# Tile 0's front of a hybrid decoder step: products of 128 and 256 columns replaced by products of 512 columns over pairs of weight chunks

## What is computed

```
mod  = silu(c) @ w_ada + b_ada                      # six rows of 1024 for each of nine conditions
h    = rmsnorm(x, g1) * (1 + scale1) + shift1
proj = h @ w_in                                     # 7 x 1024 columns: q, k, v, u, gv, gate a, gate b
out_b = stick_breaking_attention(q, k, v)           # 8 heads x 128, causal
out_a = gelu(u) * (tril(w_s) @ layernorm(gelu(gv)) + b_s)
merged = sigmoid(gate_a) * (out_a @ w_ba) + sigmoid(gate_b) * (out_b @ w_bb)
x    = x + gate1 * (merged @ w_out)
h2   = rmsnorm(x, g2) * (1 + scale2) + shift2
q2   = h2 @ w_query                                 # 8 heads, two halves of 128
s    = q2 . sub_keys  -> top 16 of each half -> best 16 of the 256 pairs = 16 experts per head
y    = rmsnorm(x + gate2 * sum_k softmax_k * gelu(h2 . down[e_k]) * up[e_k])
```

## Time and profile before

| | |
|---|---|
| median of three timed runs | 2341.11 us |
| the profiled execution: device time | 2341.77 us |
| the profiled execution: span, first to last instruction | 2340.0 us |
| mean granted TensorE clock | 0.838 |
| busy: PE, DVE, POOL, ACT | 73%, 70%, 35%, 34% |
| DMA | 841.14 MB, mean 359 GB/s |

### The profile page before, as it was taken

The page is one execution under the profiler, slowest core; times in us unless marked ns, Lnnn a source line. Parts: engine busy times, 40 slices in busy tenths (PEclk is TensorE's granted clock), DMA queues, the critical chain, the costliest instruction groups (busy, mean ns, idle before and its releaser), DMA issues.

```text
span 2340.0 us, 22796 instructions
## 1 busy us (share of the span) xinstructions
PE 1712.1 (73%) x7010; PEld 1189.8 (51%) x7010; DVE 1630.5 (70%) x3454; ACT 802.8 (34%) x2085; POOL 814.7 (35%) x647
## 2 busy tenths in 40 slices
PE   6998957988889666878777763766460677777776
PEld 2747956845778555644475752765450222222111
DVE  1011168748898878877985968888989866766764
ACT  1121013386345123238413213452122334443332
POOL 0000024324343324434433423443345444444432
PEclk9999978978989787987655586888685899999989
DMA  7786879977989979997896998999999999999997
GB/s 232 277 259 228 299 305 422 421 299 286 410 343 421 393 283 422 418 421 272 345 417 261 412 365 328 375 420 369 363 412 354 390 420 420 421 415 416 378 387 300
DMA packets 129310, 841.14 MB, mean 359 GB/s; under 512 B 15487, under 2 KB 20863, under 8 KB 33882
## 3 DMA queue, kind: packets, MB, share of 16 engines
q0 software_dynamic: 86512, 615.29, 65.3%
q1 hardware_dynamic: 37348, 217.83, 24.8%
q10 hardware_dynamic: 5328, 6.56, 0.8%
HBM read 824.39 MB, written 15.22 MB: 359 GB/s over the span
## 4 chain that ended last, share of the span: by engine, by line
DMA 28%; PE 27%; DVE 22%; ACT 8%; issue 7%; DVEq 5%; ACTq 1%; POOL 1%; SPq 0%; POOLq 0%
DMA gather_ring<-in_experts,expert_numbers 27%; PE bank L749 10%; PE bank L740 8%; DVE gather_ring L1575 7%; DVE expert_sums L1588 7%; PE bank L763 4%; PE bank L1003 3%; ACT L1234 1%; ACT L1091 1%; POOL gather_ring L672 1%; ACT expert_coefs L1238 1%; ACTq L1088 1%; DVEq L1538 1%; DVEq L1551 1%; ACT expert_acts L1234 1%
## 5 line engine op out<-in xcount | busy, mean ns | idle before, releaser
L672 POOL DMA_INDIRECT gather_ring<-in_experts,expert_numbers x576 | 781.0, 1356 | 1486.1 <-DVE expert_sums L1588 810.8
L1588 DVE SCALAR_TENSOR_TENSOR expert_sums<-gather_ring,expert_coefs,expert_sums 128x1024 f32<-128x1024 f32 x378 | 483.3, 1279 | 98.1 <-ACT expert_coefs L1238 96.3
L1575 DVE CUSTOM_DVE_ANT_0 gather_ring<-gather_ring,h_kept 128x1024 f32<-128x1024 f32 x384 | 468.4, 1220 | 90.7 <-DMA gather_ring<-in_experts,expert_numbers 89.7
L1003 PE MATMUL bank<-gather_ring,expert_sums 128*128 128x512 f32 (+1 forms) x768 | 386.3, 641 | 187.6 <-ACT expert_sums L1252 187.3
L1234 ACT ACTIVATE expert_acts<-expert_dots 128x1 f32<-128x1 f32 x576 | 116.4, 202 | 1026.7 <-DVE expert_dots L1575 1023.5
L749 PE MATMUL bank<-hT,weight_chunks 128*128 128x128 f32 (+2 forms) x2304 | 419.7, 345 | 56.5 <-ACT sigmoids L1164 18.1
L749 PEld LDWEIGHTS bank<-hT,weight_chunks 128*128 128x128 f32 x2304 | 384.6, 204 | 87.2 <-ACT qT L1142 14.5
L1003 PEld LDWEIGHTS bank<-gather_ring,expert_sums 128*128 128x128 f32 (+1 forms) x768 | 127.3, 181 | 446.2 <-ACT expert_sums L1252 240.6
L1575 DVE CUSTOM_DVE_ANT_0 gather_ring<-gather_ring,u_and_gv 128x1024 f32<-128x1024 f32 x192 | 234.3, 1223 | 147.7 <-DMA gather_ring<-in_experts,expert_numbers 147.3
L740 PE MATMUL bank<-weight_chunks,hT 128*128 128x256 f32 (+1 forms) x960 | 229.2, 401 | 23.8 <-ACT u_and_gv L1147 10.6
L740 PEld LDWEIGHTS bank<-weight_chunks,hT 128*128 128x128 f32 (+1 forms) x960 | 181.2, 191 | 68.5 <-issue 29.3
(11 more groups left out here) (206 smaller groups left out, 1753.5 us busy)
## 6 DMA issues: line engine op xcount, KB each, us to landing
weight_chunks<-in_w_in SPq DMA_DIRECT2D x84, 1024.0 KB
weight_chunks<-in_w_ada SPq DMA_DIRECT2D x24, 1024.0 KB
weight_chunks<-in_w_query SPq DMA_DIRECT2D x24, 1024.0 KB
weight_chunks<-in_w_branch_a SPq DMA_DIRECT2D x12, 1024.0 KB
weight_chunks<-in_w_branch_b SPq DMA_DIRECT2D x12, 1024.0 KB
weight_chunks<-in_w_out SPq DMA_DIRECT2D x12, 1024.0 KB
gather_ring<-in_experts,expert_numbers POOLq DMA_INDIRECT x576
u_and_gv<-in_cache_k SPq DMA_DIRECT2D x16, 512.0 KB, 10.9
```

What stands on the lines that cost most here:

```text
L672: pool.indirect_dma_start(out=ring[:, item % RING, :], out_offset=None, in_=experts, in_offset=bass.IndirectOffsetOnAxis(ap=expert[:, seq( ...
L1003: mm = nc.tensor.matmul(bank[b + half][0:n, :], by[:, r % KEPT, :], up[:, half * 512:(half + 1) * 512], start=(k == 0), stop=(k == TOPK * ...
L1575: nc.vector.tensor_tensor_reduce(out=down, in0=down, in1=h2_of(t), scale=1.0, scalar=0.0, op0=ALU.mult, op1=ALU.add, accum_out=dots[:, c:c ...
L1588: nc.vector.scalar_tensor_tensor(out=a, in0=up, scalar=coef[:, c:c + 1], in1=a, op0=ALU.mult, op1=ALU.add).then_inc(s_vsum, 1)
```

## The change

Only tile 0's front changes; fronts 1 and 2 and all rows stay as they were. Its weights come as 36 pairs of chunks (512 columns, 2 MB). Three pairs are buffered: one in two of the three chunk buffers, two in the gather slots 3 to 6, which are free until the rows begin. Every product of this front is token-major with 512 moving columns, `wide(p, src)`: eight per pair. Where the next product needs channels by tokens (q, u, merged, queries), the rows are copied out by ACT or DVE and turned by `turn_four`, and ACT copies them again: ten more turns of four. The first modulation part is five pairs instead of eight chunks, the rest seven. The silu waits only for the two condition loads (`s_c`). The merge runs gate a, gate b, then branch b, before it needs the gated u. SP's order of loads is rewritten; both u pairs and the first gv pair are asked for before the attention. ACT carries out the whole front, all queries and scores with it, before `exponentials(0)`. `STRETCH_AT[0]` becomes -5.0, and the clock no longer counts front 0: front(1)'s first piece is due at row 1.8, its first query piece at row 112.6 and its last at 128.7; nothing changes in the rows per piece. POOL waits with ring slots 3 to 6 until the last pairs in them are used. The diff, cut to its core:

```diff
+WIDE = 2 * WC
+FIRST_MODS = 5
+NADA = NMOD * D // WIDE
...
+        for key, pairs in (("first", FIRST_MODS), ("q", 2), ("k", 2), ("v", 2), ("rest", NADA - FIRST_MODS), ("u", 2),
+                           ("gv", 2), ("merge", 8), ("out", 2), ("query", 4)):
+            self.fills[key, 0] = self.fill
+            self.fill += pairs
+        self.pairs = self.fill
...
-STRETCH_AT = [CLOCK["query", g, 5] for g in range(3)]
+STRETCH_AT = [-5.0] + [CLOCK["query", g, 5] for g in range(1, 3)]
...
+        c9 = acc[0:NG, 1, :]
+        g1row = h2keep[0:NG, 1, :]
         g2row = acc[0:NG, 0, :]
+        pairs = [wbuf[:, 0:2]] + [flat[:, s * 2 * D:(s + 2) * 2 * D].rearrange("p (c k n) -> p c k n", c=2, k=KC)
+                                  for s in (3, 5)]
...
+        sg_wide = sg[:, :, :].rearrange("p a n -> p (a n)").rearrange("p (a n) -> p a n", a=2)
...
+            def load_pair(p, name, at):
+                if p >= 3:
+                    f = p - 3
+                    sp.wait_ge(s_full[f % 4], f // 4 + 1)
+                for c in range(2):
+                    sp.dma_start(pairs[p % 3][:, c], wv[name][at // WC + c]).then_inc(s_pair[p % 3], 16)
+            def load_pairs(phase, name, at, which):
+                for p in which:
+                    load_pair(fill_base(0, phase) + p, name, at + p * WIDE)
...
-            sp.dma_start(c9[0:1, :], c_prompt).then_inc(s_cond, 16)
-            sp.dma_start(c9[1:NG, :], c_sample).then_inc(s_cond, 16)
-            load_phase(0, "first", "ada", 0, range(WBUF))
-            load_x(0, s_x[0])
+            sp.dma_start(c9[0:1, :], c_prompt).then_inc(s_c, 16)
+            sp.dma_start(c9[1:NG, :], c_sample).then_inc(s_c, 16)
+            load_pairs("first", "ada", 0, range(1))
             sp.dma_start(mod9, b_ada.broadcast_to([NG, NMOD * D])).then_inc(s_cond, 16)
             sp.dma_start(g1row, g_norm1.broadcast_to([NG, D])).then_inc(s_cond, 16)
+            load_x(0, s_x[0])
+            load_pairs("first", "ada", 0, range(1, 3))
             sp.dma_start(g2row, g_norm2.broadcast_to([NG, D])).then_inc(s_cond, 16)
             sp.dma_start(ws_nat, w_spatial.rearrange("l g t s -> t (l g) s")).then_inc(s_small, 16)
             sp.dma_start(sk_nat, sub_keys.rearrange("l a k d -> k (l a) d")).then_inc(s_small, 16)
@@ -525,9 +571,57 @@
             sp.dma_start(bsb[:].rearrange("p g t -> p (g t)"),
                          b_spatial.rearrange("l g t -> l (g t)").broadcast_to([P, NH * P])).then_inc(s_small, 16)
             sp.dma_start(pt_sb[:], page_table.rearrange("(o b) n -> o (b n)", o=1)).then_inc(s_pt, 16)
-            load_phase(0, "first", "ada", 0, range(WBUF, FIRST_MODS))
+            load_pairs("first", "ada", 0, range(3, FIRST_MODS))
...
+            load_pairs("q", "in", 0, range(2))
+            load_pairs("k", "in", D, range(2))
+            load_pairs("v", "in", 2 * D, range(2))
+            load_table(0, "gv", "")
+            load_table(0, "bv", "")
+            load_pairs("rest", "ada", FIRST_MODS * WIDE, range(1))
+            evacuated(sp, fill_base(0, "v"))
+            sp.dma_start(nkp[0], gvt(0)).then_inc(s_kst, 16)
+            load_pairs("rest", "ada", FIRST_MODS * WIDE, range(1, 4))
+            evacuated(sp, fill_base(0, "rest"))
+            sp.dma_start(nvp[0], values_of(0)).then_inc(s_vst, 16)
+            load_pairs("rest", "ada", FIRST_MODS * WIDE, range(4, NADA - FIRST_MODS))
+            load_pairs("u", "in", 3 * D, range(2))
+            load_pairs("gv", "in", 4 * D, range(1))
+            evacuated(sp, fill_base(0, "u"))
+            sp.wait_ge(s_mod, 2)
+            sp.dma_start(mod_p[:, 2 * D:], mod9[0:1, 2 * D:]).then_inc(s_modst, 16)
+            sp.dma_start(mod_s.rearrange("(b i) n -> b i n", i=DSEQ)[:, :, 2 * D:],
+                         mod9[1:NG, 2 * D:].unsqueeze(1).broadcast_to([NDEC, DSEQ, 4 * D])).then_inc(s_modst, 16)
+            load_pairs("gv", "in", 4 * D, range(1, 2))
+            merge = [("in", 5 * D), ("in", 6 * D), ("bb", 0), ("ba", 0),
+                     ("in", 5 * D + WIDE), ("in", 6 * D + WIDE), ("ba", WIDE), ("bb", WIDE)]
+            for p, (name, at) in enumerate(merge):
+                load_pair(fill_base(0, "merge") + p, name, at)
+                if p == 0:
+                    sp.wait_ge(s_vst, 16)
+                    sp.wait_ge(s_modst, 32)
+                    load_x(0, s_xr[0])
+                    load_table(0, "G1", "p")
+            load_table(0, "A2", "p")
+            load_table(0, "B2", "p")
+            load_pairs("out", "out", 0, range(2))
+            load_pairs("query", "query", 0, range(3))
+            evacuated(sp, fill_base(0, "query"))
+            sp.dma_start(x1_dram[0], xbuf[:, 0, :]).then_inc(s_x1st, 16)
+            load_pairs("query", "query", 0, range(3, 4))
+            sp.wait_ge(s_x1st, 16)
+            sp.wait_ge(s_n2h, 1)
+            load_x(1, s_x[1])
...
+                    if item >= 3:
+                        f = last_pair((item - 1) // 2)
+                        pool.wait_ge(s_full[f % 4], f // 4 + 1)
...
+            def wide(p, src):
+                pe.wait_ge(s_pair[p % 3], 32 * (p // 3 + 1))
+                w, out = pairs[p % 3], take(p)
                 for k in range(KC):
-                    mm = nc.tensor.matmul(out[0:NG, 0:WC], cT[:, k, :], w[:, k, :], start=(k == 0), stop=(k == KC - 1))
-                mm.then_inc(s_full[f % 4], 1)
+                    mm = nc.tensor.matmul(out[0:src.shape[2], :].rearrange("p (c n) -> p c n", c=2), src[:, k, :], w[:, :, k, :],
+                                          start=(k == 0), stop=(k == KC - 1))
+                mm.then_inc(s_full[p % 4], 1)
+            def turn_row(t, row, half):
+                turn_four(t, [row[:, (4 * half + j) * P:(4 * half + j + 1) * P] for j in range(4)])
...
+            def wide_then_turn(phase, src, p, key, row, half, ready):
+                wide(fill_base(0, phase) + p, src)
+                evacuated(pe, ready)
+                turn_row(turn_base(0, key) + half, row, half)
+            for p in range(2):
+                wide(fill_base(0, "q") + p, h)
+            for p in range(2):
+                wide_then_turn("k", h, p, "qT", q_rows, p, fill_base(0, "q") + p + 1)
+            for p in range(2):
+                wide_then_turn("v", h, p, "kT", gvt(0), p, fill_base(0, "k") + p + 1)
+            for p in range(NADA - FIRST_MODS):
+                wide(fill_base(0, "rest") + p, cT)
+            turned(pe, turn_base(0, "uT"))
+            evacuated(pe, fill_base(0, "u"))
+            attention(0)
+            for p in range(2):
+                wide(fill_base(0, "u") + p, h)
+            for p in range(2):
+                wide_then_turn("gv", h, p, "uT", u_rows, p, fill_base(0, "u") + p + 1)
+            merge = fill_base(0, "merge")
+            wide(merge, h)
+            wide(merge + 1, h)
+            wide(merge + 2, q)
+            pe.wait_ge(s_lnh, 1)
+            for half in range(2):
+                turn = turn_base(0, "gate") + half
+                out = take_turn(turn)
+                for j in range(4):
+                    gr = 4 * half + j
+                    mm = nc.tensor.matmul(out[:, j * P:(j + 1) * P], gvt(0)[:, gr * P:(gr + 1) * P], WsT[:, gr, :],
+                                          start=True, stop=True)
+                mm.then_inc(s_tfull[turn % 2], 1)
+            turned(pe, turn_base(0, "mT"))
+            wide(merge + 3, u)
+            wide(merge + 4, h)
+            wide(merge + 5, h)
+            evacuated(pe, merge + 4)
+            turn_row(turn_base(0, "mT"), m_rows, 0)
+            wide(merge + 6, u)
+            wide(merge + 7, q)
+            evacuated(pe, fill_base(0, "out"))
+            turn_row(turn_base(0, "mT") + 1, m_rows, 1)
+            turned(pe, turn_base(0, "norm2"))
+            for p in range(2):
+                wide(fill_base(0, "out") + p, m)
+            pe.wait_ge(s_n2h, 1)
+            for half in range(2):
+                turn_row(turn_base(0, "norm2") + half, h2_of(0), half)
+            turned(pe, turn_base(0, "query"))
+            def turn_queries(p):
+                evacuated(pe, fill_base(0, "query") + p + 1)
+                turn_four(turn_base(0, "query") + p, [query_rows(p)[:, j * P:(j + 1) * P] for j in range(4)])
+            wide(fill_base(0, "query"), h)
+            turn_queries(0)
+            pe.wait_ge(s_qh, 1)
+            key_scores(0, 0)
+            for p in range(1, 4):
+                wide(fill_base(0, "query") + p, h)
+                if p == 1:
+                    pe.wait_ge(s_qh, 2)
+                    key_scores(0, 1)
+                else:
+                    for c in (2 * p - 2, 2 * p - 1):
+                        pe.wait_ge(s_qh, c + 1)
+                        key_scores(0, c)
+                turn_queries(p)
+            for c in (NH - 2, NH - 1):
+                pe.wait_ge(s_qh, c + 1)
+                key_scores(0, c)
+            pe.wait_ge(s_sev[0], NH)
...
```

(70 more changed lines are left out.)

379 lines of the change are left out of this document (242 added, 137 removed).

## The result

The changed kernel takes 2356.6 us (median of four runs, 2355.89 to 2358.3) against 2342.02 for the kernel before beside it: ratio 1.0063, 95% interval 1.005 to 1.0075. It is slower by 14.6 us. The forecast was 2339 with a range up to 2350. The profiled execution has a span of 2356.6 us, 16.6 more than before.

What follows compares the result with a forecast made beforehand. PE was taken to pace front 0 and, with front(1)'s chain, tile 0's rows. Front 0's -24.2 us became a 32 us lead, spent on query pieces (+3.6); tile 1's first rows gave -5.8: net -2.2, 2339 us, range 2318 to 2350.

Steps and rivals of the forecast that it cites:

- Queries at 279: End of front 0: its queries start at 279 us instead of 303.1, with 275 to 286 as range.
- part 1: Front 0, from the start to its queries: savings sum to -24.2 us, with bounds of -4 to +7.
- Query start to first dot: From front 0's first query product through ACT's tail and the normalizations to tile 0's first dot: 56.7 us.
- The slower rival: End of front 0's queries: stores take 11.8 us, ACT and DVE end 8 us later, 2347 us; chance 0.12.
- The faster rival: Front(1) takes less than 443.8 us as waits and some clock loss go, 17 us, giving 2322; chance 0.26.
- First query product to the end of the last add: End of tile 0: front(1)'s first query product at 790, the last add at 848 us.
- the fourteen pieces: Front(1)'s query pieces ahead of tile 0's last coefficient: per two, 6.9 us of products and 1.0 of scores, 56 us.
- Tile 1's first rows: Start of tile 1, now without those query pieces beside its rows: 44.5 us instead of 50.2, -5.8.
- part 3: From front(1) to the end: last add +3.6 us, tile 1's first rows -5.8, net -2.2.
- the store: Store of head 4's scores, which holds head 6's copy: taken as 7 us (3 to 12), bounds -4 to +9.
- the last rows: The last rows' term in the forecast's error bounds: -3 to +3 us.
- the lead of front(1): Front(1)'s products start at 346 instead of 378.20, 32 us earlier, spent on ten more query pieces inside tile 0's rows.

Runs made afterwards that it cites:

- e5: The changed kernel with six buffers instead of two for group 0's scores, so that no copy waits for a store: 2351.5 us, ratio 1.0035.
- e1: The changed kernel with STRETCH_AT[0] = -43 instead of -5, so front(1) is due at row 11.3 again: 2350.4 us, ratio 1.0034.
- e2: The changed kernel with exponentials(0) moved ahead in ACT's program, behind the turned queries of the second pair: 2344.3 us, ratio 1.0007.
- e4: The kernel before, with its narrow front 0, but all queries carried out before exponentials(0) and front(1) due at row 1.8: 2370.1 us, ratio 1.0122.

## Why the prediction was wrong

The mechanism stood, its sum did not. Forecast was -2.2 us for the span, measured +16.6; the sums themselves hold to 0.4 us. The terms, in the order of the prediction:

- Queries at 279, measured 284.65: +5.7. The start made 2.5 of it: five pairs ended at 47.5 for 45. The first pair came at 9.4 and took 8.38 us for 6.9, the second came 1.5 late. The q phase made another 3.1: the first three pairs behind PE's idle 2.6 us took 23.69 us (chain above) where 20.6 were due, and in 54.3 to 60.4 the granted clock was 0.53. I had taken off the slow first products of the old q phase (16.42 for 128 records, granted clock 0.67 in its first 6.1 us, behind 2.4 us of idling) and given the new one none. The rest of part 1 was right to a microsecond: u and gv 28.6 for 28.5, gv's end to the last merge product 59.7 for 59.8. The tail behind it took 3.0 us.
- Query start to first dot 58.6, forecast 56.7: +1.9. The first pair took the 9.1 forecast. The stores took 9.7, 6.9 and 7.5 us from their issue to the copy that they held, where I had 7. The slower rival had the right place with too high a price: by its own condition it needed stores of some 11 us, and e5 prices the waits at 5 to 7 us. My reason for 7, that the DMA carries four gathers and little else then, was wrong. It was full:

```profile
313.50:323.30 9.80, 8.51 (x29) 4.28 (x27) 0.00 (x0) 1.57 (x6) 2.17 (x3) 1.00 1.02 421
323.70:331.20 7.50, 1.90 (x8) 1.45 (x8) 0.00 (x0) 1.02 (x3) 0.00 (x0) 0.67 1.00 414
```

- First dot to front(1) 11.0 for 10.5: +0.5.
- Front(1) 447.4 for 443.8: +3.6. The faster rival, that it would shrink, is refuted by every run in the table (443.7 to 450.7). The kernel before, whose 443.8 I took, has all but the lowest value of the twelve. PE's waits for DVE's `h_kept` in this stretch grew from 14.6 to 18.9 us, but that the 3.6 come from there is not tested.
- First query product to the end of the last add 63.6 for 58: +5.6. The other four runs with front(1) due at row 1.8 have 60.1 to 63.8 too, so the 56 us for the fourteen pieces were too few. The first copy came 6.6 us behind the product and the fourteenth piece at 861.7, 60 us behind it for 56. Most of this is in the row at 844.91: a query chunk came 2.0 us late, and the chunk behind the wait ran in 8.86 for 7.07. Its load stands in the chain with 18.43 us:

```profile
826.43 18.43 DMA weight_chunks<-in_w_query
```

The DMA was full then (share 1.02, 381 GB/s from 826 to 845). In the kernel before, three of these chunks were asked for from 845.9 on, in the gap between the tiles, with no gather issued until 864.3 and the DMA at 219 GB/s; now they lie beside rows.
- Tile 1's first rows 46.5 for 44.5: +2.0. The gap between the tiles was 28.3, as forecast.

Together 19.3, against 18.8 between -2.2 and +16.6. None of these terms is large, and none came out shorter.

The step that failed is the sum at the end of part 3, where I set a gain of 32 us against a cost of nearly the same size; the mis-sized terms in it are the query start (+5.7), front(1) (+3.6) and the last query pieces (+5.6). I had given a bound to three terms, +7 for part 1, +9 for the store and +3 for the last rows. They measured +5.7, +1.9 and +2.0, all inside, and by themselves bring the time to some 2349, still inside the range. What carried it out are the terms without a bound: front(1), taken at the length that one trace showed, and the fourteen pieces, taken at their undisturbed time though their loads now lie beside rows. Together with the half microsecond at the first dot they make 9.7 us. These terms stand in series on one chain, so nothing on another engine could take them up. The rival for faster, 0.26 of the 0.45, rested on waits that the profile showed inside front(1) itself, and a new start did not remove them: 10.4 us for the attention weights (9.9 before) and 5.9 for the chunk (5.3).

What was right: the lead of front(1) counts and not the first dot alone (e1 and e2), though the part of the rows in the stretch stays open as said above; the lead is spent on ten more query pieces; the width by itself is worth about nothing; POOL's new wait does not matter. In the changed kernel it held back four gathers, the last of which went out at 322.0, 21 us before the first dot.

## What to carry to other kernels

When a front is woven into another tile's work by position, a faster front gives nothing until the hand-over is looked at: list what the first waiting instruction of the next stage stands behind on each engine (here one `exponentials(0)` at the end of ACT's program, and three waits for stores ahead of it), and count how many pieces stand ahead of the last instruction that the stage after needs. Cost such a chain with the stalls it will have, not with undisturbed times, and give every term of it a bound, those that "stay the same" too: here a gain and a cost of the same size were subtracted, and six of the seven small omissions came out on the same side, the seventh at nothing. And try the single waits first: one semaphore for two loads gave 5 to 7 us, the width of the products about 1.

## What the runs showed of the hardware

SP's issue of the table of short pieces held it from 6.59 to 21.06 in the changed kernel, against 5.16 us before the change. Ahead of it stood six weight chunks of 1 MB, where there were three before the change:

```profile
6.59 14.43 SPq L569 DMA_DIRECT2D sigmoids<-in_sub_keys  x1
...
22.38 0.80 SPq L522 DMA_DIRECT2D weight_chunks<-in_w_ada  x2
```

The DMA was full meanwhile (share 1.01, 335 GB/s). An issue can thus block its queue for long; that it waits until earlier transfers have drained fits the two lengths, but no run tested it. The fourth pair, asked for at 22.4 and not at 17.8 when its buffer came free, arrived only 0.4 us late for PE. Where ACT waited for a store of 128 KB at the end of front 0's queries, it took 6.9 to 10.8 us from its issue, with the DMA full each time (414 to 421 GB/s in the changed kernel, 397 to 424 in e4). How long it takes on an idle DMA no run shows.
